# A hybrid attention and expert layer on one core: attention units taken two by two on TensorE

## The reference

```python
def _stick_breaking(q, k, v, q_pos, k_pos):          # per block of 128 query rows
    z = jnp.einsum('bqhd,bkhd->bhqk', qi, k).astype(jnp.float32) * scale
    valid = (k_pos[None, :] < pi[:, None])[None, None]
    log_beta = jax.nn.log_sigmoid(z)
    log_1m = jnp.where(valid, jax.nn.log_sigmoid(-z), 0.0)
    suffix = lax.cumsum(log_1m, axis=3, reverse=True) - log_1m
    a = jnp.where(valid, jnp.exp(log_beta + suffix), 0.0)
    return jnp.einsum('bhqk,bkhd->bqhd', a.astype(v.dtype), v)

def _layer(x, c, ...):                               # once for 1024 prompt rows, once for 64 sample rows
    hn = (_norm(x) * (1 + sc1) + sh1).astype(x.dtype)
    u, q, k, v = jnp.split(hn @ w_in, ...)           # 512 columns each; 8 heads of 64
    pool_out, new_pool = _pool_mixer(u, hist_pool, past, w_pool, pool_scale)
    attn = _stick_breaking(q, k_all, v_all, q_pos, k_pos)   # the sample has 512 rows of cache ahead
    mix = jnp.concatenate([pool_out, attn], axis=-1) @ w_out
    x = _layer_norm(ALPHA * x + (1 + g1) * mix, ln1_g, ln1_b)
    hn2 = (_norm(x) * (1 + sc2) + sh2).astype(x.dtype)
    ff = _moe(hn2, ...)                              # 16 experts, two for each row
    return _layer_norm(ALPHA * x + (1 + g2) * ff, ln2_g, ln2_b), k, v, new_pool
```

## Time and profile before

| | |
|---|---|
| median of 3 runs | 871.09 us |
| the three runs | 874.38, 867.37, 871.09 us |
| the profiled execution, first to last instruction (span) | 865.4 us |
| mean granted TensorE clock of that span | 0.974 |
| TensorE busy in it | 794.0 us, 92% |
| VectorE busy in it | 596.8 us, 69% |
| ScalarE busy in it | 350.4 us, 40% |
| first score of unit 0 | 242.28 us |
| last value product, unit 55 | 497.26 us |
| end of `block_b`'s work on TensorE | about 535 us |

### The profile page before, as it was taken

The page is one execution under the profiler, slowest core; times in us unless marked ns, Lnnn a source line. Parts: engine busy times, 40 slices in busy tenths (PEclk is TensorE's granted clock), DMA queues, the critical chain, the costliest instruction groups (busy, mean ns, idle before and its releaser), DMA issues. The chain is left out here.

```text
span 865.4 us, 13448 instructions
## 1 busy us (share of the span) xinstructions
PE 794.0 (92%) x4805; PEld 624.0 (72%) x4806; DVE 596.8 (69%) x685; ACT 350.4 (40%) x645; POOL 305.9 (35%) x259
## 2 busy tenths in 40 slices
PE   2899999999988899999999995499999999999894
PEld 2689999999955555676767784278888888888641
DVE  6679579752078965776777566998556999572087
ACT  3811111111155763444454435435454445453144
POOL 3000799950000010100000001157565787453156
PEclk9999999999999999999999998699999999999997
DMA  8956543630073401310202036888878997889493
GB/s 320 397 175 203 173 153 128 188 98 2 1 273 126 134 26 49 98 68 31 74 26 73 25 122 238 282 320 274 282 262 310 401 391 262 309 303 350 182 369 142
DMA packets 77362, 165.32 MB, mean 191 GB/s; under 512 B 7397, under 2 KB 32517, under 8 KB 75266
## 3 DMA queue, kind: packets, MB, share of 16 engines
q1 hardware_dynamic: 68402, 132.15, 43.8%
q0 software_dynamic: 7760, 28.31, 9.1%
q10 hardware_dynamic: 1152, 4.19, 1.5%
HBM read 132.57 MB, written 32.08 MB: 190 GB/s over the span
## 5 line engine op out<-in xcount | busy, mean ns | idle before, releaser
L2099 PE MATMUL psum<-we_hi,x_parts 128*128 x384 | 137.4, 403 | 1.5 <-DVE we_lo L1722 1.1
L1722 DVE TENSOR_TENSOR we_lo<-we_raw,we_hi 128x2048 fp32r<-128x2048 f32 x48 | 116.2, 2424 | 1.5
L1721 DVE CAST we_hi<-we_raw 128x2048 fp32r<-128x2048 f32 x44 | 60.1, 1365 | 46.8 <-DMA we_raw<-in_w_down_dram 24.0
L449 PE MATMUL psum<-hn_hi,w_hi 128*128 128x364 f32 (+1 forms) x384 | 90.7, 331 | 1.3 <-issue 0.7
L449 PE MATMUL psum<-hn_lo,w_hi 128*128 128x364 f32 (+1 forms) x384 | 90.1, 329 | 0.0
L449 PE MATMUL psum<-hn_hi,w_lo 128*128 128x364 f32 (+1 forms) x384 | 89.8, 328 | 0.0
L2099 PEld LDWEIGHTS psum<-we_hi,x_parts 128*128 128x128 f32 x384 | 72.1, 188 | 16.6 <-issue 2.3
L1040 PE MATMUL psum<-wo_hi,mixin 128*128 128x512 f32 (+1 forms) x256 | 83.4, 397 | 0.0
L2099 PE MATMUL psum<-we_lo,x_parts 128*128 x192 | 75.2, 392 | 0.0
L633 DVE SCALAR_TENSOR_TENSOR proj<-wm,cT,proj 128x2048 f32<-128x2048 f32 x28 | 72.5, 2638 | 0.0
L449 PEld LDWEIGHTS psum<-hn_hi,w_hi 128*128 128x128 f32 x384 | 66.9, 189 | 5.7 <-issue 4.8
(11 more groups left out here) (334 smaller groups left out, 1582.2 us busy)
## 6 DMA issues: line engine op xcount, KB each, us to landing
we_raw<-in_w_up_dram SPq DMA_DIRECT2D x32, 1024.0 KB, 9.3
wm<-in_w_mod_dram SPq DMA_DIRECT2D x16, 1024.0 KB, 5.6
we_raw<-in_w_down_dram SPq DMA_DIRECT2D x16, 1024.0 KB, 6.9
w_raw<-in_w_in_dram SPq DMA_DIRECT2D x16, 512.0 KB, 6.3
we_raw<-ff_d SPq DMA_DIRECT2D x12, 512.0 KB, 8.1
proj<-in_x_prompt_dram SPq DMA_DIRECT2D x4, 1024.0 KB, 8.0
sc_room<-in_w_mod_dram SPq DMA_DIRECT2D x4, 1024.0 KB, 14.3
proj<-in_w_mod_dram SPq DMA_DIRECT2D x2, 2048.0 KB, 12.1
```

What stands on the lines that cost most here:

```text
L449: mm = pe.matmul(psum[:, 3 * slot + c, 0:n], w[:, slot, k, :], hn[:, k, t0:t0 + n], start=(k == 0 and w is w_hi and hn is hn_hi), stop=(k ...
L1721: then(dve.tensor_copy(we_hi[:, a:b], raw))
L1722: dve.tensor_tensor(we_lo[:, a:b], raw, we_hi[:, a:b].bitcast(F32), ALU.subtract).then_inc(ready, 1)
L2099: mm = pe.matmul(psum[:, bank, :], x[:, s, k, :], w[:, bass.ds(at + k * 2 * DE, 2 * DE)], start=(k == 0 and x is x_hi and w is we_hi), sto ...
```

## The change

TensorE takes the units of `block_b` in rounds of two. Round k (slots 2k and 2k+1) now holds both scores of units 2k and 2k+1, then both value products of units 2k-4 and 2k-3, then the turn of unit 2k-2 with the other work of slot 2k behind it, and the turn of unit 2k-1 with the other work of slot 2k+1 behind it. ScalarE takes `sticks(2k+1)` ahead of the other work of slot 2k. VectorE takes both `copy_att` of units 2k-4 and 2k-3 behind `weights(2k)`. Where a pair of heads has one unit alone (units 8 to 23), the odd unit's value product goes to bank 5, which head 1 of the turns uses too; the turns then wait for its copy. The low parts of `w_out` (`wl`) are spread over slots 13 to 23, where they had slots 12 to 19.

```diff
 DVE_BESIDE = {
-    2: "TV:0", 3: "DV:0", 5: "TV:1", 7: "TV:2", 9: "TV:3", 10: "TV:4", 12: "TV:5 wl:0", 13: "wl:1 TV:6 wl:2",
...
+    2: "TV:0", 3: "DV:0", 5: "TV:1", 7: "TV:2", 9: "TV:3", 10: "TV:4", 12: "TV:5", 13: "wl:0",
...
+        def att_bank(u):
+            return 5 if units[u][5] and units[u][6] and u % 2 else 6
+        def bank_read(u):
+            q = units[u][7]
+            return max((v[7] + 1 for w, v in enumerate(units[:u]) if v[7] < q and att_bank(w) == att_bank(u)), default=0)
...
                 for h in range(2):
                     if u >= 1:
                         pe.wait_ge(aT_copied, 2 * u - 1 + h)
+                    if h and u >= LAG and att_bank(u - 1 - u % 2) == 5:
+                        pe.wait_ge(att_copied, units[u - 1 - u % 2][7] + 1)
...
-                if top and q:
-                    pe.wait_ge(att_copied, q)
+                if top and bank_read(u):
+                    pe.wait_ge(att_copied, bank_read(u))
...
-            for u in range(nu + LAG + 1):
-                if u < nu:
-                    scores(u)
-                if 0 <= u - LAG < nu:
-                    turn(u - LAG)
-                if u > LAG:
-                    values(u - LAG - 1)
...
+            for u in range(0, nu + LAG, 2):
+                two = (u, u + 1)
+                if u < nu:
+                    scores(u)
+                    scores(u + 1)
+                if u >= 2 * LAG:
+                    values(u - 2 * LAG)
+                    values(u - 2 * LAG + 1)
...
+                for w in two:
+                    if w >= LAG:
+                        turn(w - LAG)
+                    if w == nu + LAG - 1:
+                        values(nu - 2)
+                        values(nu - 1)
+                    others(w)
+            others(nu + LAG)
...
+            for u in range(0, nu + LAG, 2):
+                if u < nu:
+                    sticks(u)
+                if u >= LAG:
+                    copy_aT(u - LAG)
...
+                if u < nu:
+                    sticks(u + 1)
+                others(u)
+                if u >= LAG:
+                    copy_aT(u + 1 - LAG)
...
+                others(u + 1)
...
                 if u < nu:
                     weights(u)
-                if u > LAG and units[u - LAG - 1][6]:
-                    copy_att(u - LAG - 1)
+                if u % 2 == 0 and u >= 2 * LAG:
+                    for before in (u - 2 * LAG, u - 2 * LAG + 1):
+                        if units[before][6]:
+                            copy_att(before)
```

More of the change, by code:

```diff
@@ L1027, in values @@
                         c = p * P + 64 * h
-                        mm = pe.matmul(psum[64 * h:64 * h + 64, 6, 0:r], v[:, c:c + 64], aT[0:m, s, h, b, 0:r],
+                        mm = pe.matmul(psum[64 * h:64 * h + 64, att_bank(u), 0:r], v[:, c:c + 64], aT[0:m, s, h, b, 0:r],
                                        start=(top and b == 0), stop=(bottom and b == nb - 1))
@@ L1079, in _, with others @@
                 turn_v(n)
-            for u in range(nu + LAG + 1):
-                if u < nu:
-                    scores(u)
-                if 0 <= u - LAG < nu:
-                    turn(u - LAG)
-                if u > LAG:
-                    values(u - LAG - 1)
-                if u < 2:
-                    for n in ((4, 5, 6), (7, 8))[u]:
-                        turn_v(n)
+            def others(u):
                 if u == nu + LAG:
@@ L1108, in _ @@
                         router(n)
+            for u in range(0, nu + LAG, 2):
[6 more added lines that the diff above has]
+                    values(u - 2 * LAG + 1)
+                if u == 0:
+                    for n in range(4, TILES):
+                        turn_v(n)
+                for w in two:
[6 more added lines that the diff above has]
+            others(nu + LAG)
         @block.scalar
@@ L1220, in _ @@
                         copy_h(n, int(step[1]))
+            for u in range(0, nu + LAG, 2):
[3 more added lines that the diff above has]
+                    copy_aT(u - LAG)
+                if u == 0:
+                    stage_v(5)
+                if u < nu:
[3 more added lines that the diff above has]
+                    copy_aT(u + 1 - LAG)
+                if u == 0:
+                    stage_v(7)
+                others(u + 1)
+            others(nu + LAG)
         @block.vector
@@ L1274, in copy_att @@
                 dve.wait_ge(pv_done, u + 1)
-                dve.tensor_scalar(proj[:, 4 + p, i * P:i * P + r], psum[:, 6, 0:r], vlast[:, p, i:i + 1], None,
+                dve.tensor_scalar(proj[:, 4 + p, i * P:i * P + r], psum[:, att_bank(u), 0:r], vlast[:, p, i:i + 1], None,
                                   ALU.add).then_inc(att_copied, 1)
```

## The result

The changed kernel takes 871.78 us (median of nine runs, 869.98 to 872.77); the kernel before, in nine runs beside it, 868.51. The ratio of the runs is 1.0028 with a 95% interval of 1.0014 to 1.0041: 2.4 us slower, between 1.2 and 3.6. The two medians stand 3.3 us apart. This is far less than 1%, but it is a small loss clear of the noise. The profiled executions differ by 2.8 us, 865.4 and 868.2. The prediction had +3.7 us on a base of 871.09.

A forecast was written before the change was run, and what follows sets the result against it. TensorE was taken to bound units 26 to 55, hand-overs between TensorE and VectorE units 12 to 24. Terms: -5.4 - 0.3 - 3.2 + 8.0 + 4.6 = +3.7 us, from 871.09 to 874.8, range 861 to 884.

The forecast's parts named there:

- term 4: Units 4 to 25: earlier scan of unit 12, then a new loop in rounds 6 to 11 through `copy_att`; +4.6 us.
- rival B: New waits don't form, ScalarE and VectorE keep up: 862 us, or 860 if bank 5's wait never binds; chance 0.18.
- Term 1: TensorE, units 26 to 55: rounds of two save entries of 0.35 us a round, -5.4, and two turn entries, -0.3.
- term 3: Units 26 to 55: new TensorE waits for readers of bank 7, mostly ScalarE; +8.0 us, between 3 and 11.
- the base: Time before the change, the median of the runs shown, 871.09 us, to which the +3.7 was added.
- goes through to the end: Tail, 498 to 537 us: it starts with products TensorE bounds, so a shift there reaches the end whole.
- Term 2: Units 26 to 55: value products no longer wait for `copy_att` behind VectorE's scan; -3.2 us.
- C: Second score and value product of a pair each pay the whole entry: 880.2 us, chance 0.08; load alone 877.2, 0.05.
- D: TensorE's clock runs at the lower level for half of rounds 6 to 11: +7.5, 882.3 us; chance 0.12.

The follow-up runs named there:

- one_bank_two_places: The changed kernel with all values in bank 6, an odd single unit's in other columns, so turns wait for no `copy_att`: 860.85 us.
- both_copy_first: The changed kernel with one_bank_two_places' edit, ScalarE's old order and, in VectorE's slot 44, the copy of `M0:4` ahead of `B1:3`: 854.80 us, again 854.18.

## Why the prediction was right and wrong

**The steps that failed.** The worst is the price of the new wait for bank 5, in term 4 and rival B: some 5 us as part of the loop, "a further 2" if it never binds. Taking it away gave 10 us of the early stretch. Term 1 was too small by 1.8 us, since turns too lost an entry, and term 3 by 2.2. In the sum, the base and the claim that a shift "goes through to the end" failed. The number came out near the measured one partly by luck, as errors cancelled.

**The total.** The sign (a small loss, within 1%) and the range held. The size was high: +3.7 us was forecast and +2.4 (1.2 to 3.6) measured, or 3.3 between the medians. Two steps failed for the number as a time. First the base: the three runs shown had a median of 871.09, nine have 868.51, so that 874.8 was 2.6 us high before any term was counted. The 5.7 us between median and span were mostly that too: in each of the changed kernel's nine runs the time is 1.7 to 1.8 us above the run's own span. Second, "a shift at its start goes through to the end". The shift at slot 58 was +3.5 us (498.29 to 501.78), close to the 3.7. At the last logits of the tail it was 4.8 (535.07 to 539.85), at the next block's first product 3.3 (543.86 to 547.18), and at the end 2.8. The idle time ahead of that first product, in the kernel before and, behind it, in the changed one:

```profile
543.86 0.41 PE L2012 MATMUL psum<-both,ones 128*128 128x16 bf16 x9 [8.42 <-DVE both L1653]
```

```profile
547.18 0.41 PE L2047 MATMUL psum<-both,ones 128*128 128x16 bf16 x9 [6.74 <-DVE both L1688]
```

It waits for VectorE's routing work, not for the last logits alone, and its shorter wait took back part of the shift; why VectorE was late by less is open. The nine runs can't tell 2.8 from 3.5.

**Term 4, the early loop: right for its end point, wrong in what it is made of.** Forecast: scan of unit 12 at 271.9, of unit 24 at 318.4, score of unit 26 at 323.7. Measured: 271.67, 318.64, 323.89. Round by round: 5.77, 7.17, 7.91, 9.06, 8.49, 8.57 for 6.15, 6.55, 7.75, 9.05, 8.55, 8.5. The waits of the turns were forecast at 0.7 to 1.4 us a round; four were, and those of rounds 7 and 9 were 2.5 and 2.9. The forecast also read all of VectorE's 2.5 us of idle time ahead of unit 12 as late scores; for 0.7 us of it VectorE waited for `TV`. But the forecast took the loop's price as the difference to before, some 5 us, and gave rival B "a further 2 back" if the wait didn't bind. That is the step that failed most. Without the wait the early stretch is 10 us shorter (41.73 against 51.78). The chain of a round was added up with care and its alternative not at all: what VectorE alone would need in rounds 6 to 11 is its busy time, 35 us, against 46.5. The wait cost 10 there, the rounds of two and the spread `wl` had brought 4.4 (46.10 to 41.73), and only the sum was seen.

**Term 1, the entries: under-sized.** The price held, 0.20 and 0.14 for 0.20 and 0.15, and 15 rounds were worth 4.3 to 4.9 us (two tests) for 5.25. But TensorE's busy time in the main stretch fell by 8.6 (181.46 to 172.88), and with the pairs taken apart it was still 3.2 under before (178.27). Of these, 1.1 and 0.5 are no saving: the score of unit 25 lies in the stretch before, ahead of it after, and half in it with the pairs apart (124, 120 and 122 score records). That leaves 7.5 for a forecast of 5.7, and 2.7 that the pairs do not explain. "They save no turn entry where other work stands between the turns" was the wrong step. Eight blocks of a turn take 1.03 us ahead of a value product and 0.82 ahead of a mix product (357.98 to 358.80); the first mix product then takes 0.31 to the next, where later ones take 0.23. Together that is 1.13, and eight blocks at 0.11 with one mix product are 1.11: the passage costs next to nothing. A mix product takes 0.23 ahead of a turn as well (449.12 to 449.35) and 0.32 ahead of a score. Before, the other work stood between a value product and a score:

```profile
345.26 0.44 PE L1028 MATMUL psum<-aT_room,dv 128*64 128x128 f32 x4 [0.57 <-DVE proj L1275]
345.63 0.50 PE L1040 MATMUL psum<-wo_hi,mixin 128*128 128x512 f32 x1
345.97 0.39 PE L1040 MATMUL psum<-wo_lo,mixin 128*128 128x512 f32 x1
```

There four value records take 0.37, 0.15 more than four times 0.055, and the first mix product 0.34: some 0.26 for the passage. A turn and a mix product both use the full 128 by 128 tile, a value product 64 columns of it and a score 64 rows. That accounts in kind for the 2.7; no run isolated it.

**Term 2** (3.2 us of waits for `copy_att`): gone, as forecast; its worth was not isolated.

**Term 3, the new waits: right place, a little too small.** Forecast 8.0 us (its own items add up to 8.3, which the sum should have carried), listed by the profile 10.2. `M0:2` 1.5 for 1.6, `R:0` and `M0:6` 1.4 each for 1.6 and 1.8, the last value product 0.9 for 1.1. Missed was `T2:1` behind `C0:4`, 1.7: the forecast held that a turn covers VectorE's readers of bank 7, but here the reader is queued behind `B1:3`. Undoing ScalarE's order was worth 4.1 to 5.3 us, the one swapped copy 1.3 to 1.5. Terms 1 to 3 came to -0.9 in the forecast and term 4 to +4.6. Split in the same way, the traces give +4.8 for term 4 (the score of unit 26 at 323.89 for 320.12, and value product 22 behind it) and -1.3 for the others, up to slot 58. This is close by luck: two errors cancel, a saving missed in term 1 and a wait in term 3.

**Rivals.** B's conditions were made true one after the other: without the wait for bank 5 the time is 860.85, and without most of the waits of term 3 as well 854.98, where the forecast had 860 to 862 for both (857 to 859 on the base of nine runs). C fell: the second score of a pair takes 0.86 us. The Trainium skill's TensorE: Matmul & The Clock Gate, Part 3, "The mechanism", says in its list of what overlaps that a weight load overlaps matmuls in flight only when its row group differs. In the text above that list it also lets a load go ahead when it is for the background weight buffer. The prediction was wrong that the scores put this to the test: a score's first head uses rows 0 to 63 and its second rows 64 to 127, so the second score's first load differs in rows from the matmul ahead of it. Nor do the turns: a block takes 0.11 us for 128 columns, twice the pace of a score's 512 columns in 0.21. The value products do. All use the same 128 rows, each record has a load of its own, and the second product's 12 records take 0.66 us, 0.055 each, which is a score's pace: the trace goes against the first sentence and is open to the second.

D did not come in its size. It had TensorE at the lower level for half of rounds 6 to 11; the granted clock there was 0.96, as before the change. Without the wait it was 1.00 in `one_bank_two_places`, and 0.96 in `both_copy_first`, whose early stretch is only 0.6 us longer. The clock's share in the 10 us is at most 2.4 by TensorE's busy time.

## What to carry to other kernels

When a change adds a wait on a reader in another engine's queue, look at what stands ahead of that reader: a copy behind a scan of the same round made a chain of score, sigmoid, scan, copy and turn out of engines that had overlapped. Price the wait against what the busiest engine alone would need, not against the time before, or a gain and a loss cancel unseen. And when work is regrouped, list for every shared buffer which engine frees it, and what is now queued ahead of that.

## What the runs showed of the hardware

The entry price fits the change of tile better than the change of the instruction's kind: between a turn and a mix product, both full tiles, next to nothing (1.13 us for work of 1.11), between a value product and a mix product some 0.26, and 0.09 more from a mix product to a score than to a turn (0.32 and 0.23). The weight loads of value products that follow each other on the same 128 rows were hidden (0.055 us a record). And the same early stretch took 41.36 us at a granted clock of 1.00 and 42.34 at 0.96, in the profiles of two kernels that differ only from slot 44 on.
